# Seven-product gate and up projections in a two-layer trunk, with the weight sums on VectorE

## The chip, the cores and the metric

One core of a Trainium2 chip runs the whole kernel. The metric is the device time of one execution in microseconds; for one core that is its own time. A run's profile gives the span from the first to the last instruction.

## What is computed

A trunk of two layers on 512 tokens with 16 learned meta tokens in front (528 rows of 1024 features, float32). Layer 0 mixes by a state-space scan and a gated linear unit (GLU), layer 1 by windowed attention. Behind each mixer stands a feed-forward network, and it is the object here:

```python
def swiglu_ffn(h, w_gate, w_up, w_down):
    return (jax.nn.silu(h @ w_gate) * (h @ w_up)) @ w_down
# h: (528 or 512, 1024); w_gate, w_up: (1024, 2816); w_down: (2816, 1024)
h_res = h_res + swiglu_ffn(rms_norm(h_res, ln_ffn[i]), w_gate[i], w_up[i], w_down[i])
```

Layer 0 runs it on 528 tokens, layer 1 on 512, since the meta tokens aren't needed behind the attention.

## The kernel before

Activations lie transposed: features on the 128 partitions, tokens along the free dimension. A feature matrix of 1024 rows is 8 blocks of 128. Float32 precision is kept by splitting each operand into a rounded part ("high") and the rest ("low"), and each block product is three matmuls: high x high, low x high and high x low.

**Weights.** SyncE loads a tile of 256 weight columns (all 8 blocks of rows, 1 MB) into one of two buffers `raw` (`load_tile`, line 377; the issue is line 381). ScalarE rounds 128 columns of it into `w_high` (`round_weights`, line 580), VectorE subtracts to make `w_low` (`split_weights`, line 940). Both hold two sets of 128 columns, so the rounding of a set waits until TensorE has finished with the product that used it two products before. SyncE loads a tile when the one before in its buffer is split.

**A quad** is four products: two of gate, two of up (128 output features each). `product` (line 1367) runs over 8 row blocks, three matmuls each; in layer 0 the 528 tokens are cut into 256 and 272 columns in two PSUM banks, in layer 1 a matmul takes all 512. The innermost lines:

```python
for k in range(w_k, w_k + nk):
    for w, xx in ((high, xh), (high, xl), (low, xh)):
        for h, (c0, cn, b0) in enumerate(parts):
            ins = nc.tensor.matmul(banks[:, bank + h, b0:b0 + cn], w[:, j, k, :], xx[...])
```

Feed-forward has 11 quads per layer, in a hardware loop (TensorE lines 1649 to 1660; the layer's input waits are in `first_quad`, line 1633). VectorE (`up`, line 1217) multiplies the gate product by the row of inverse norms, ScalarE (line 812) applies SiLU, GpSimd (line 562) multiplies it by the inverse norm again, for the up product, VectorE multiplies that by the up product out of PSUM. The result is rounded by ScalarE (line 823) and split by VectorE (line 1233) into `a_high`, `a_low`, which hold all 22 blocks.

**The down products** (`down`, lines 1661, 1236 and 825) then give 8 blocks of 128 output features, two at a time, each over the 22 blocks of rows, in four tiles of weights; at the end VectorE adds the product to the residual, and `updated` (lines 776 and 1166) makes the next normed input's high and low parts and the square that the norm needs. The last block of layer 1 is done in two token halves, each with its own addition, scaling and square, and the output transposes follow (lines 1612 to 1631).

**The norm** is taken after the product: `mean` and `spread` (lines 1594 and 1603) are two small groups of matmuls between the first products of a stage; the inverse norm's row is copied out by ScalarE (line 806).

In front of layer 0's feed-forward stand the GLU's four quads (lines 1188 and 1191 multiply and add to the residual). In front of layer 1's stands the output projection of the attention, 8 blocks of 24 matmuls of 512 columns, each followed on VectorE by the addition (line 1351), a weight split and `updated`.

## Time and profile before

| | |
|---|---|
| median of 3 runs | 1182.28 us (1181.73 to 1182.97) |
| span of the profiled execution | 1177.9 us; its own time stands on no page, the median is 4.4 us above the span |
| TensorE busy | 1140.4 us, 97% |
| VectorE busy | 553.8 us, 47% |
| ScalarE busy | 412.4 us, 35% |
| GpSimd busy | 174.8 us, 15% |
| mean granted clock of TensorE | 0.994 |

Matmuls are pipelined: a matmul's length in the trace is its latency, and what it costs is the distance to the next one's start. "Busy" of TensorE is the time in which one is under way. The chain is followed back from the last instruction, at each step to what released it.

### The profile page before, as it was taken

The numbers are of one execution on the slowest core, as the hardware profiler recorded it, in microseconds if no ns is written. First come the engines' busy times: TensorE is split into PE (matmuls) and PEld (weight loads), VectorE is DVE, ScalarE is ACT, GpSimd is POOL, SyncE is SP. The second block draws the span as 40 slices with busy tenths as digits, with TensorE's granted clock in tenths as the row PEclk, the third lists the DMA queues.
The fourth block names the chain that finished last, engine by engine and source line by source line (L and its number), as shares of the span: only waits on it lengthen the run. The fifth ranks groups of instructions, "written<-read, shape, count | busy, mean of one in ns | idle before, by whom it ended". The sixth has DMA issues, their size and how long they took to land.

```text
span 1177.9 us, 20443 instructions
## 1 busy us (share of the span) xinstructions
PE 1140.4 (97%) x8362; PEld 1025.8 (87%) x8362; DVE 553.8 (47%) x845; ACT 412.4 (35%) x701; POOL 174.8 (15%) x114
## 2 busy tenths in 40 slices
PE   5799999999999999999999899989999999999998
PEld 5688899999999999999999676678888888888887
DVE  7978444443344333444334355455443434434444
ACT  6823232332222222233323455443322223223332
POOL 4699000011111111100000000001111111110000
PEclk9999899999999999999999999999999999999999
DMA  7164333222323232222323211022333233223332
GB/s 141 24 163 111 87 109 108 72 89 91 98 80 100 78 107 71 76 83 91 98 81 126 72 37 42 32 72 72 108 107 99 79 107 107 75 73 97 98 98 94
DMA packets 119387, 104.63 MB, mean 89 GB/s; under 512 B 21868, under 2 KB 117216, under 8 KB 119008
## 3 DMA queue, kind: packets, MB, share of 16 engines
q1 hardware_dynamic: 110120, 99.85, 27.9%
q10 hardware_dynamic: 9216, 4.06, 1.5%
q8 instruction: 37, 0.61, 0.2%
q14 instruction: 14, 0.11, 0.0%
HBM read 98.11 MB, written 5.24 MB: 88 GB/s over the span
## 4 chain that ended last, share of the span: by engine, by line
PE 90%; DVE 4%; DMA 2%; ACT 1%; POOL 1%; issue 1%; SPq 0%; ACTq 0%; DVEq 0%; POOLq 0%
PE banks L1380 79%; PE banks L1520 1%; PE banks L1457 1%; PE banks L1510 1%; PE banks L1731 1%; PE banks L1734 1%; PE banks L1752 1%; PE banks L1721 1%; PE banks L1458 1%; DMA y_dram<-y_act 1%; PE banks L1746 1%; PE banks L1472 0%; POOL col_mag L499 0%; PE banks L1720 0%; ACTq L719 0%
## 5 line engine op out<-in xcount | busy, mean ns | idle before, releaser
L587 ACT CAST w_high<-raw 128x1024 fp32r<-128x1024 f32 x186 | 195.0, 1049 | 572.1 <-PE banks L1380 572.1
L945 DVE TENSOR_TENSOR w_low<-raw,w_high 128x1024 fp32r<-128x1024 f32 x186 | 228.2, 1228 | 208.3 <-ACT w_high L587 208.3
L1380 PE MATMUL banks<-x_high,w_high 128*128 128x512 f32 (+2 forms) x1184 | 321.0, 324 | 1.0 <-DVE x_low L1173 1.0
L1380 PE MATMUL banks<-x_high,w_low 128*128 128x512 f32 (+2 forms) x1184 | 318.5, 322 | 0.0
L1380 PE MATMUL banks<-x_low,w_high 128*128 128x512 f32 (+2 forms) x1184 | 317.7, 321 | 0.0
L1380 PEld LDWEIGHTS banks<-x_high,w_high 128*128 128x128 f32 x1184 | 198.9, 189 | 19.4 <-issue 2.2
L1380 PEld LDWEIGHTS banks<-x_low,w_high 128*128 128x128 f32 x1184 | 198.9, 188 | 16.1
L1380 PEld LDWEIGHTS banks<-x_high,w_low 128*128 128x128 f32 x1184 | 198.2, 188 | 16.8
L1380 PE MATMUL banks<-a_high,w_high 128*128 128x256 f32 (+2 forms) x533 | 141.2, 318 | 0.0
L1380 PE MATMUL banks<-a_low,w_high 128*128 128x256 f32 (+2 forms) x533 | 141.1, 318 | 0.0
L1380 PE MATMUL banks<-a_high,w_low 128*128 128x256 f32 (+2 forms) x533 | 141.1, 318 | 0.0
L562 POOL TENSOR_TENSOR gate<-gate,rstd_row 128x528 f32<-128x528 f32 (+1 forms) x44 | 79.3, 1802 | 389.9 <-ACT gate L819 389.9
L1380 PEld LDWEIGHTS banks<-a_low,w_high 128*128 128x128 f32 x533 | 89.3, 188 | 6.8
L1380 PEld LDWEIGHTS banks<-a_high,w_high 128*128 128x128 f32 x533 | 89.3, 188 | 6.7
L1380 PEld LDWEIGHTS banks<-a_high,w_low 128*128 128x128 f32 x533 | 89.2, 188 | 6.6
L1230 DVE TENSOR_TENSOR prod<-banks,gate 128x528 f32<-128x528 f32 (+1 forms) x44 | 30.8, 700 | 131.7 <-PE banks L1380 131.7
L1224 DVE TENSOR_TENSOR gate<-banks,rstd_row 128x528 f32<-128x528 f32 (+1 forms) x44 | 30.6, 699 | 127.8 <-PE banks L1380 120.0
L553 POOL TENSOR_TENSOR rstd<-mean_sq,neg_half 88x6 f32<-88x6 f32 (+1 forms) x3 | 3.7, 1225 | 447.8 <-DVE mean_sq L1201 447.8
L1380 PE MATMUL banks<-glu_high,w_high 128*128 128x256 f32 x224 | 47.6, 294 | 0.7 <-DVE glu_low L1124 0.7
L1380 PE MATMUL banks<-glu_low,w_high 128*128 128x256 f32 x224 | 46.7, 290 | 0.0
L1380 PE MATMUL banks<-glu_high,w_low 128*128 128x256 f32 x224 | 46.4, 289 | 0.0
L1380 PEld LDWEIGHTS banks<-glu_high,w_high 128*128 128x128 f32 x224 | 36.0, 193 | 1.5 <-DVE glu_low L1124 0.9
(288 smaller groups left out, 1249.3 us busy)
## 6 DMA issues: line engine op xcount, KB each, us to landing
raw<-in_ffn_w_gate SPq DMA_DIRECT2D x22, 1024.0 KB, 5.3
raw<-in_ffn_w_up SPq DMA_DIRECT2D x22, 1024.0 KB, 5.3
raw<-in_ffn_w_down SPq DMA_DIRECT2D x16, 768.0 KB, 4.4
raw<-in_ffn_w_down SPq DMA_DIRECT2D x16, 640.0 KB, 4.1
raw<-in_attn_w_qkv SPq DMA_DIRECT2D x6, 1024.0 KB, 5.0
k_toep<-k_dram SPq DMA_DIRECT2D x64, 64.0 KB, 2.6
raw<-in_ssm_w_glu_b SPq DMA_DIRECT2D x4, 1024.0 KB, 5.5
raw<-in_ssm_w_glu_a SPq DMA_DIRECT2D x4, 1024.0 KB, 5.8
```

The costliest lines, as they stand in the source:

```text
L562: nc.gpsimd.tensor_tensor(gate[:, j, a:e], gate[:, j, a:e], rstd_row[:, a:e], ALU.mult).then_inc(gate_scaled, 1)
L587: nc.scalar.copy(high[:, j], raw[:, slot, :, j * P:(j + 1) * P]).then_inc(w_rounded, 1)
L945: nc.vector.tensor_tensor(low[:, j], raw[:, slot, :, j * P:(j + 1) * P], high[:, j], ALU.subtract).then_inc(w_split, 1)
L1224: TT(tokens_of(gate[:, j], n), bank_view(2 * j, n), tokens_of(rstd_row[:], n), ALU.mult).then_inc(pre_ready, 1)
L1230: TT(tokens_of(prod[:, j], n), bank_view(4 + 2 * j, n), tokens_of(gate[:, j], n), ALU.mult).then_inc(up_taken, 1)
L1380: ins = nc.tensor.matmul(banks[:, bank + h, b0:b0 + cn], w[:, j, k, :], xx[:, first_k + k, c0 + base:c0 + base + cn], start=start and k == ...
L1457: nc.tensor.matmul(o, inj[:, r_, i].rearrange("p t q -> p (t q)"), ident[:], start=True, stop=False)
L1458: ins = nc.tensor.matmul(o, inj_t[:, r_, 1 - i].rearrange("p t q -> p (t q)"), (ident if i else neg_ident)[:], start=False, stop=True)
L1510: nc.tensor.matmul(banks[:, 6 + j, r_ * C:(r_ + 1) * C], k_toep[:, b % 2, 2 * r_ + j, :], u_state[:, b * GB + 2 * r_ + j, :], start=True, ...
L1520: ins = nc.tensor.matmul(banks[:, 6 + j, r_ * C + 1:(r_ + 1) * C], read[hs, b % 3, r_, i, 1:T + 1].rearrange("p t q -> p (t q)"), state[hs ...
L1721: ins = nc.tensor.matmul(o[:, META:], q, keys[:, first:first + BAND], start=True, stop=True)
L1731: nc.tensor.transpose(banks[0:w, 6, i * P:(i + 1) * P], prob_b[:, s % 2, i, 0:w], ident[:])
```

## The change

The gate and up products use a seven-product scheme (Strassen's, in Winograd's form). A unit is now 256 weight columns of gate or of up. The weights' row blocks are taken in four pairs, the columns in two blocks of 128, the tokens in two halves (264 or 256), so that each unit is a 2 x 2 by 2 x 2 product of blocks. It takes seven part products of half the tokens instead of eight. Each part is 4 slots x 3 matmuls of 264 or 256 columns.

- Of the weights: five forms of a unit are split into high and low: the first column, S2, the pair S3 and S1, the corner, S4. The four sums are made by VectorE on 512 elements per partition each, two of them in place in `raw`. `raw` has five blocks per pair for it; a unit is loaded by two DMAs of 512 KB.
- Of the inputs: seven forms of each pair of input blocks (`xs_high`, `xs_low`), made as each residual block is ready (`pair_first`, `pair_second`): VectorE makes four differences T1 to T4, ScalarE rounds and VectorE splits all seven.
- Of the results: parts are added by accumulation in PSUM; in between ScalarE copies three states of a bank to SBUF, and VectorE makes three corners from these copies and banks. TensorE waits for a copy before parts 3, 5 and 6 and for a corner before part 7.
- GpSimd's scaling of the gate is gone: VectorE scales the pre-activation by the inverse norm, and the down product once more by it (`scale_down`).
- Activations are kept in 5 slots instead of 22, so the down products are done in three stages (pairs 0 to 2, 3 to 6, 7 to 10), behind 4, 8 and 11 gate and up pairs; each stage adds to the residual. A down unit has two products, with as many matmuls per layer as before. The last unit of layer 1 is done in quarters (two blocks, two token halves).
- The first unit of each layer is prepared while the stage in front of it runs: in layer 0 during the last GLU quad, in layer 1 behind output block 5 (sums and three splits), 6 and 7.
- ScalarE's and VectorE's loops over the quads are written out.

The core of the diff:

```diff
-DOWN_TILES = ((0, 6), (6, 6), (12, 5), (17, 5))
+STAGES = ((0, 3), (3, 7), (7, 11))
+SLOTS = 5
+UPS = ((0, 4), (4, 8), (8, 11))
...
+            def part(w, i, x, slots, c, bank, n, start=False, need=None):
+                for m, slot in enumerate(slots):
+                    if need is not None:
+                        need(m)
+                    for a, b in ((0, 0), (0, 1), (1, 0)):
+                        ins = nc.tensor.matmul(bank_part(bank, n), w[a][:, m, i, :], x[b][:, slot, c, :],
+                                               start=start and m == 0 and a == b, stop=m == len(slots) - 1 and a == 1,
+                                               skip_group_check=not start)
+                ins.then_inc(part_done, 1)
+            def summed_unit(g, ups, downs, parity, x, n, first=False, spread_at=None, mean_at=None, need_b11=None, need_all=None):
+                y, w, v = Y_BANK[parity], W_BANK[parity], X_BANK[parity]
+                forms, slots = 5 * ups + 2 * downs, range(KP)
+                if need_b11 is None and spread_at is None:
+                    pe.wait_ge(set_free, g - 1)
+                pe.wait_ge(t_split, forms + (4 if first else 1))
+                part(col, 0, x, slots, B11, y, n, start=True, need=need_b11)
...
+                part(col, 1, x, slots, B21, v, n, start=True, need=need_all)
+                pe.wait_ge(t_split, forms + (4 if first else 2))
+                pe.wait_ge(part_copied, 3 * ups + 1)
+                part(w2, 0, x, slots, T2, y, n)
...
+                pe.wait_ge(t_split, forms + (5 if first else 3))
+                part(sums, 0, x, slots, T3, w, n, start=True)
+                pe.wait_ge(part_copied, 3 * ups + 2)
+                part(sums, 1, x, slots, T1, y, n)
+                pe.wait_ge(t_split, forms + (5 if first else 4))
+                pe.wait_ge(part_copied, 3 * ups + 3)
+                part(w2, 1, x, slots, T4, w, n)
+                pe.wait_ge(t_split, forms + 5)
+                pe.wait_ge(c22_made, ups + 1)
+                part(w2, 2, x, slots, B22, y, n)
...
+            def sum13(g, kp):
+                TT(w[:, :, 2, :], w[:, :, 4, :], w[:, :, 1, :], ALU.add).then_inc(sums_made, 1)
+                dve.wait_ge(sums_made, 2 * ups_before(g) + 1)
+                TT(w[:, :, 1, :], w[:, :, 1, :], w[:, :, 0, :], ALU.add).then_inc(sums_made, 1)
...
+                TT(s24[:, 0, 0:kp], w[:, :, 0, :], w[:, :, 2, :], ALU.add).then_inc(s2_made, 1)
...
+                TT(s24[:, 1, 0:kp], blocks_of(g, kp)[:, :, 3, :], s24[:, 0, 0:kp], ALU.add).then_inc(s4_made, 1)
...
+                def gate_unit(i, behind):
+                    g, kp = UNITS * layer + up_unit(i), KP
+                    sum2(g + 1, kp)
+                    sum4(g + 1, kp)
...
+                    first_corner(g, gate_part(n, 0, 0))
...
+                    split_column(g + 1, kp)
+                    if behind:
+                        split_acts(i - 1)
+                    split_s2(g + 1, kp)
+                    last_corner(g, gate_part(n, 1, 1))
...
+                    split_sums(g + 1, kp)
+                    low_corner(g, gate_part(n, 1, 0))
...
+                    dve.wait_ge(part_done, parts_before(g) + 7)
+                    TT(gate_part(n, 0, 1), bank_part(Y_BANK[g % 2], n), rstd_part(n, 1), ALU.mult).then_inc(set_free, 1)
+                    dve.wait_ge(c21_made, ups_before(g) + 1)
+                    TT(gate_part(n, 0, 0), gate_part(n, 0, 0), rstd_part(n, 0), ALU.mult)
+                    TT(gate[:, 1, 0:n], gate[:, 1, 0:n], rstd_row[:, t0:L], ALU.mult).then_inc(gate_pre, 1)
+                    split_corner(g + 1, kp)
+                    split_s4(g + 1, kp)
...
+            def pair_second(layer, px, n):
+                dve.wait_ge(xp_ready, 2 * pair + 2)
+                step(STT(x_t[:, 1, 0:h], x_t[:, 0, 0:h], -1.0, x_pair[:, 1, h:n], ALU.mult, ALU.subtract))
+                TT(x_t[:, 2, 0:h], x_pair[:, 0, h:n], x_pair[:, 1, h:n], ALU.subtract)
+                TT(x_t[:, 3, 0:h], x_pair[:, 1, 0:h], x_t[:, 1, 0:h], ALU.add).then_inc(xt_ready, 1)
+                TT(low[:, px, B21:T1, :], ..., high[:, px, B21:T1, :], ALU.subtract).then_inc(xs_split, 1)
+                TT(low[:, px, T1:, :], x_t[:, :, 0:h], high[:, px, T1:, :], ALU.subtract).then_inc(xs_split, 1)
+                square_added(k + 1, n)
...
+                if m == KB - 3:
+                    sum2(UNITS, KP)
+                    sum4(UNITS, KP)
+                    split_s2(UNITS, KP, rounded=1)
+                    split_corner(UNITS, KP, rounded=2)
+                    split_s4(UNITS, KP, rounded=3)
+                if m == KB - 2:
+                    split_column(UNITS, KP, rounded=4)
+                if m == KB - 1:
+                    split_sums(UNITS, KP, rounded=5)
```

TensorE's wait `need_all` in front of each slot of part 2 is for all forms of that pair of inputs. An up unit's queue on VectorE is like the gate unit's without `split_acts`, and its last three products are by the gate. On ScalarE a unit has its three copies, the five roundings of the next unit, and in gate units the rounding of the activations behind `round_s2`, in up units the SiLU of both blocks (1056 or 1024 elements) there.

## Rows read from the trace of the kernel before

**Rows 1.** The summary of the page: busy time per engine, and shares of the chain.

```profile
PE 1140.4 (97%) x8362; PEld 1025.8 (87%) x8362; DVE 553.8 (47%) x845; ACT 412.4 (35%) x701; POOL 174.8 (15%) x114
...
PE 90%; DVE 4%; DMA 2%; ACT 1%; POOL 1%; issue 1%; SPq 0%; ACTq 0%; DVEq 0%; POOLq 0%
```

**Rows 2.** Busy us per engine in stretches of both up stages; then granted clock and DMA.

```profile
250.00:484.00 234.00, 234.00 (x1925) 234.00 (x1925) 91.22 (x101) 65.42 (x83) 38.88 (x22) 1.00 0.28 89
...
830.00:1040.00 210.00, 210.00 (x928) 173.91 (x927) 86.19 (x97) 62.08 (x78) 35.48 (x20) 1.00 0.30 94
```

**Rows 3.** The chain in order of time: start us, us, what.

```profile
247.76 380.39 PE banks L1380 x3120
...
773.76 38.38 PE banks L1380 x168
...
819.41 348.45 PE banks L1380 x1551
```

**Rows 4.** Timeline of TensorE in the last product: start us, us, line, shapes.

```profile
1164.33 0.28 PE L1380 MATMUL banks<-a_high,w_low 128*128 128x256 f32 x1
...
1167.57 0.28 PE L1380 MATMUL banks<-a_high,w_low 128*128 128x256 f32 x1
```

**Rows 5.** Groups by shape of VectorE: count, busy us, mean ns, idle before.

```profile
L945 DVE TENSOR_TENSOR w_low<-raw,w_high 128x1024 fp32r<-128x1024 f32 x186 | 228.2, 1228 | 208.3 <-ACT w_high L587 208.3
...
L1224 DVE TENSOR_TENSOR gate<-banks,rstd_row 128x528 f32<-128x528 f32 x22 | 15.5, 707 | 68.0 <-PE banks L1380 63.9 <-ACT rstd_row L806 4.0
...
L1087 DVE TENSOR_TENSOR nat_b_im<-nat_b_im,lam_t 128x512 f32<-128x512 f32 x1 | 0.7, 693 | 0.0
...
L1137 DVE TENSOR_TENSOR banks<-banks,zt 128x260 f32<-128x260 f32 x8 | 3.5, 437 | 0.3
```

**Rows 6.** Timeline of VectorE in the opening part.

```profile
35.50 0.69 DVE L1087 TENSOR_TENSOR nat_b_im<-nat_b_im,lam_t 128x512 f32<-128x512 f32 x1
36.23 0.69 DVE L1088 TENSOR_TENSOR nat_b_im<-nat_b_im,turn_t 128x512 f32<-128x512 f32 x1
...
37.10 1.22 DVE L1100 TENSOR_TENSOR inj<-banks,nat_b_re 128x1024 f32<-128x1024 f32 x1
38.23 1.22 DVE L1102 TENSOR_TENSOR inj_t<-banks,nat_b_im 128x1024 f32<-128x1024 f32 x1
```

**Rows 7.** Timeline around the end of the GLU products.

```profile
232.34 0.41 PE L1380 MATMUL banks<-x_high,w_high 128*128 128x256 f32 x2
...
232.54 0.71 DVE L1188 TENSOR_TENSOR prod<-banks,gate 128x528 f32<-128x528 f32 x1 [2.79 <-PE banks L1380]
...
233.28 1.27 DVE L1191 TENSOR_TENSOR residual<-residual,prod 128x528 f32<-128x528 f32 x1
...
238.64 0.51 PE L1380 MATMUL banks<-x_high,w_high 128*128 128x256 f32 x2 [0.99 <-DVE x_low L1173]
```

**Rows 8.** Groups by shape of ScalarE.

```profile
L587 ACT CAST w_high<-raw 128x1024 fp32r<-128x1024 f32 x186 | 195.0, 1049 | 572.1 <-PE banks L1380 572.1
...
L890 ACT CAST o_high<-banks 128x256 fp32r<-128x256 f32 x16 | 6.0, 375 | 2.2 <-PE banks L1752 2.2
...
L823 ACT CAST a_high<-prod 128x512 f32 x20 | 12.3, 617 | 0.2 <-issue 0.2
```

**Rows 9.** A DMA issue of the page: KB each, median us to landing.

```profile
raw<-in_ffn_w_gate SPq DMA_DIRECT2D x22, 1024.0 KB, 5.3
```

**Rows 10.** Busy us in slices of 2 us in the attention; the granted clock follows POOL.

```profile
672.00:674.00 2.00, 0.00 (x0) 0.00 (x0) 0.31 (x2) 1.61 (x10) 0.00 (x0) 1.00 0.00 0
674.00:676.00 2.00, 1.12 (x10) 0.90 (x12) 1.78 (x7) 0.00 (x0) 0.00 (x0) 0.87 0.00 0
676.00:678.00 2.00, 2.00 (x10) 1.34 (x7) 0.00 (x0) 1.47 (x7) 0.00 (x0) 0.50 0.03 8
678.00:680.00 2.00, 2.00 (x9) 1.60 (x8) 0.98 (x4) 0.92 (x7) 0.00 (x0) 0.77 0.00 0
```

**Rows 11.** Timeline in the attention: the idle time before is in brackets.

```profile
674.88 0.63 PE L1731 MATMUL banks<-ident,prob_b 128*64 128x128 f32 x4 [3.05 <-DVE prob_m L1327]
```

More of the change, by code:

```diff
@@ L335, in tokens_of @@
             return ap if n == L else ap[:, META:L]
-        def layer_rows(full, short, m, n):
-            return rows(full, m, 0, L) if n == L else rows(short, m, 0, SEQ)
         def cols(ap, n):
@@ L837, in feed_forward @@
                 if layer == 0:
-                    with act.Fori(0, N_DOWN, 1) as i:
-                        down(i, False)
-                else:
-                    with act.Fori(0, N_DOWN - 1, 1) as i:
-                        down(i, False)
-                    for off in range(6):
-                        round_weights(QUAD_DOWN[layer] + 2 * (N_DOWN - 1), 2 + off)
-                    updated(adds0 + KB - 2, KB - 2, n, gain)
-                    for h in range(2):
-                        r_h = half_tokens(h)
-                        act.wait_ge(added, adds0 + KB - 1 + h + 1)
-                        nc.scalar.activation(gate[:, 0, r_h], residual[:, KB - 1, r_h], ACT.Square).then_inc(squared, 1)
@@ L851, in _ @@
-            feed_forward(0, L, N_GLU, KB, 0, "ln_mix1")
+                    for m in range(KB - 2, KB):
+                        normed(m)
+                        squared_of(KB + m, m, n)
+                else:
+                    for q in range(2):
+                        act.wait_ge(last_ready, q + 1)
+                        nc.scalar.activation(last_sq[:, :, q * h:(q + 1) * h], residual[:, KB - 2:, half_tokens(q)],
+                                             ACT.Square).then_inc(squared, 1)
@@ new lines, in plain_product @@
+            def plain_product(x, weights, slots, it0, bank, n, cut, need):
+                for m, slot in enumerate(slots):
+                    if need:
+                        pe.wait_ge(act_split, 2 * (it0 + m) + 2)
+                    for i in range(2):
+                        for a, b in ((0, 0), (0, 1), (1, 0)):
+                            for h, (c0, cn) in enumerate(cut):
+                                ins = nc.tensor.matmul(banks[:, bank + h, 0:cn], weights[a][:, m, i, :], x[b][:, slot, i, c0:c0 + cn],
+                                                       start=m == 0 and i == 0 and a == b, stop=m == len(slots) - 1 and i == 1 and a == 1)
+                ins.then_inc(part_done, 1)
@@ new lines, in plain_unit @@
+            def plain_unit(g, ups, downs, parity, x, s, layer, n):
+                p0, p1 = STAGES[s]
+                slots, it0 = [p % SLOTS for p in range(p0, p1)], N_UP * layer + p0
+                pe.wait_ge(set_free, g - 1)
+                forms = 5 * ups + 2 * downs
+                cut = ((0, TOK), (TOK, TOK)) if n == L else ((0, SEQ),)
+                for j, weights in enumerate((col, sums)):
+                    pe.wait_ge(t_split, forms + j + 1)
+                    plain_product(x, weights, slots, it0, 4 * parity + 2 * j, n, cut, need=j == 0)
@@ new lines, in last_unit @@
+            def last_unit(g, x, s, layer):
+                p0, p1 = STAGES[s]
+                slots, it0 = [p % SLOTS for p in range(p0, p1)], N_UP * layer + p0
+                pe.wait_ge(set_free, g - 1)
+                pe.wait_ge(t_split, forms_before(g) + 2)
+                for q in range(2):
+                    for j, weights in enumerate((col, sums)):
+                        plain_product(x, weights, slots, it0, 4 * (g % 2) + 2 * q + j, SEQ, ((q * SEQ // 2, SEQ // 2),), need=False)
```

784 lines of the change are left out of this document (567 added, 217 removed).

## The prediction

> **What bounds the kernel now.** I read the profile in this order. The summary first [rows 1]: TensorE is busy 97% of the span and carries 90% of the chain that ended last; VectorE is busy 47%. Then busy time by stage [rows 2]: in the gate and up products of both layers TensorE is busy 100% of the stretch, VectorE about 40%, ScalarE under 30%. Then the chain in order of time [rows 3]: one unbroken TensorE piece of 380 us covers layer 0's feed-forward (3120 matmuls, 0.1219 us each), one of 348 us covers layer 1's. Taking 30 matmuls of 256 columns at 0.120 us out of the second (27 steps in 3.24 us [rows 4]), its 1521 of 512 columns take 0.2267 us. So a matmul costs its columns at 2.4 GHz plus about 13 ns, whatever its width. No wait is left in these stages: only fewer columns help, and VectorE has room to pay for them, but how much is the question.
>
> **TensorE's part.** A unit of weights (256 columns of gate or up) costs now, in layer 0, 96 matmuls of 264 columns on average; in layer 1, 48 of 512. After: 7 parts x 4 slots x 3 = 84 of 264 or 256. Layer 0: 22 units x 12 x 0.1219 = 32.2 us less. Layer 1: 1056 x 0.2267 = 239.4 against 1848 x 0.120 = 221.8, 17.6 us less; narrower matmuls give a good part of its one eighth back. The down products keep their matmuls; the last one, cut in quarters, costs 0.4 us more. Together **-49.4 us**. Taking GpSimd's scalings of the gate away gives nothing: they lie beside a TensorE that never waits [rows 2]. Their work comes to VectorE, below.
>
> **VectorE's part, and where the queues meet.** For each unit VectorE now makes five splits (three of 512, two of 1024 elements), four sums of 512, three corners and a last product of half a row. The rows [rows 5]: 1.228 us for 1024 elements, 0.693 for 512, 0.707 for 528, 0.437 for 260. A gate unit has 17 such instructions, the splits of the activations among them, summing to 11.6 us; an up unit 15, 10.1 us. The timeline [rows 6] shows that the next one starts 1.13 us after a 1.22 us one, 0.08-0.09 early, but 0.73 after a 0.69 us one on whose result it waits. Six of the 32 wait so (the sums follow one another). A pair of units then occupies VectorE for 21.7 - 26 x 0.08 + 6 x 0.03 = 19.8 us, against TensorE's 168 x 0.1219 = 20.5 us (layer 0) and 168 x 0.120 = 20.2 (layer 1). VectorE goes from 40% to some 95%.
>
> The Trainium skill speaks against the overlap: "VectorE: DVE Perf Modes", section "The DRAIN you can't avoid", has the next instruction wait until the pipe of the one before is empty. By that rule a pair would take VectorE about 21.9 us, and the whole would be a rival below; [rows 6] say otherwise.
>
> Sums are not in the trace. Below: the 512-element row, 0.61 us apart; above: the residual addition with its permuted operand, 1.27 us for 528 elements against 0.71 [rows 7], so 1.8 times, 1.2 us each. The sums read runs of 128 like the split of row L945, which pays nothing for its gaps, so I take 0.61-0.73.
>
> I laid the three queues of a layer-0 pair beside each other (0: TensorE starts the gate unit; parts of 1.46 us; 0.2 us from a product's end to its reader as in [rows 7], 0.03 between VectorE and ScalarE; ScalarE 1.05 for 1024, 0.38 for a half row, 0.62 for 512 [rows 8]). VectorE comes 2.8 us late, because behind part 7 of the unit before it still has three half or full products and two splits. Sums until 5.6, first corner 5.5-6.0, column split until 7.1, two activation splits until 8.4, split of S2 until 9.0, and only then the corner for which part 7 waits, 8.9-9.3. Part 7 could have started at 8.8; it starts at 9.4. ScalarE rounds the corner's operand (6.5-6.9) well before. An up unit has no activation splits, so its corner comes at 18.9 where part 7 may start at 19.6: it holds nothing. So 0.6 us in each of 16 gate units (0.7 in layer 1), and 0.9-1.0 in the 4 first ones behind a down stage, whose last down unit holds 10 us of VectorE work against 8.8: **+13.9 us**. ScalarE has some 12 us of work per pair (six half-row copies, four of 1024, six of 512, two activation roundings, one SiLU of two rows), and its copies come in time. Weights land 5.3 us after issue [rows 9] and are asked for a whole unit ahead: nothing. The down units hold 5-8 us of VectorE work under 8-12 of TensorE: nothing.
>
> **The starts.** Product 2 of the first unit needs all forms of the last pair of inputs. Layer 0, from the end of the GLU products: product and residual until 2.2 (now 232.54 to 234.55 [rows 7]), VectorE's split of the sums until 3.4 and ScalarE's scaling, three differences until 4.6, ScalarE's rounding of four of them until 5.7, VectorE's split until 7.0. TensorE has work for 2.6 us: it stands 4.5. Unit 1 then waits for the spread of the norm (1.3 us, paid today too) and 1.7 for ScalarE's late copies. In all 8.3 us over the matmuls; today 15.4 us from 232.34 [rows 7] to 247.76 [rows 3] less 96 x 0.1219, 3.7 (1.0 of it the wait at 238.64). **+4.6.**
> Layer 1: the first unit's sums and three splits (4.6 us) and a pair's forms are put into VectorE's queue at output block 5 of 8; that step holds about 11 us and a block lasts 5.45 (24 x 0.2267). All behind is late: from the end of the last output block the residual addition ends at 4.3, and the last split at 9.0; TensorE stands 6.5 in two pieces. With unit 1: 9.7; today 819.41 less 812.14 [rows 3] less 24 x 0.2267, and 0.3 in front, 2.1. **+7.6.**
> Key and value products: the last normed block is ready 6.0 us after the down products (VectorE does a split and a square before the addition) where 5.1 would do: **+0.9.** The tail: both last blocks are scaled, added, squared after the last product, one half-row multiplication (0.4) and a wider square more: **+0.8.**
> Clock: after an idle stretch of TensorE of 3.05 us before 674.88 [rows 11] the granted clock was 0.87, 0.50, 0.77 in three slices of 2 us, the 0.50 being 1.2 of 2.4 GHz [rows 10]: 0.26 + 1.0 + 0.46 = 1.7 us lost. Both starts have an idle stretch of over 4 us: **+3.4.** Bounds: 0 each (the idle 1.0 us before 238.64 [rows 7] is followed by steps at full pace) to about 5 (a longer half-clock stretch).
>
> Sum: -49.4 + 13.9 + 4.6 + 7.6 + 0.9 + 0.8 + 3.4 = -18.2. The profiled span is 1177.9 us; the median of the runs is 1182.28, 4.4 more, which I leave as it is: **1164.1 us**.
>
> **Rivals.**
> A, slower: VectorE becomes the bound of the up stages. A pair has to cost 0.8 us more than the 21.1 (20.8 in layer 1) laid out above and the gain is gone (22 x 0.83 = 18.2); that is VectorE work 8% dearer, 0.05 us on each of 32 instructions. Its place is the corner before part 7, and the waits before it. At 10% dearer the same layout gives 22.3 and 22.1 a pair: +24, 1188 us. For it: instructions in today's trace are mostly alone, the new ones follow one another with two or three waits each. Against: [rows 6]. 0.18.
> B, slower: VectorE instructions in a row do not overlap in the new stages, each starts when the one before has ended: 22.0 and 21.8 a pair, +20, 1184 us. 0.06: [rows 6] contradict it. This is what the rule of the Trainium skill named above would make of the kernel.
> C: VectorE has slack after all, the holds at part 7, half of the starts and the clock's loss vanish: 1164.1 - 13.9 - 7 - 3.4 = 1140; half of that 1152. For it: a handover 0.5 us shorter anywhere in front of the corner ends the hold. 0.08.
> D: no change, 1180 to 1184.7: A in a weaker form. 0.06. That the change doesn't do what it says has no room: the matmuls are written out.
> The forecast: 0.62.
>
> **Numbers.** A measurement of this kernel can tell 0.2%, 2.4 us. Faster: forecast and C, 0.70; same: D, 0.06; slower: A and B, 0.24. The range runs from C's half way, 1150, to a little beyond A, 1190; beyond it lie the whole of C and dearer sums (at 1.2 us each, 2 x 22 x 4 sums x 0.5 = 88 us). The likeliest case alone: 1157 to 1174.
>
> **What would show it.** A unit's seven parts 1.46 us apart in layer 0 and 1.44 in layer 1; VectorE busy over 90% in the up stages; TensorE's idle time in front of part 7 of gate units, released by the corner; idle stretches of 4 us at both starts with a halved clock behind them; pairs of 21.1 and 20.8 us. Wrong would be: pairs over 21.9, idle time in front of other parts, sums over 0.75 us, matmuls more than 0.122 us apart.

## The result and the profile after: 1172.7 us, a gain of 0.7% where 1.5% was forecast

The changed kernel takes 1172.74 us (median of 8 executions, 1163.79 to 1176.3) against 1181.15 (8 executions, 1174.65 to 1182.97): ratio 0.9932, 95% interval 0.9903 to 0.9961, 8.4 us less. The forecast was 1164.1, 18.2 less. The profiled execution took 1163.79 us, nearly the forecast; it is the fastest of the eight, so this agreement is chance, and the account below shows what hid in it. One further execution of before (1196.64 us at a clock of 0.976) ran in a slower state and is left out below.

The summary of the page after, which answers to [rows 1], then busy time in the same two stretches as [rows 2] (columns: TensorE, its weight loads, VectorE, ScalarE, GpSimd, granted clock, DMA share, GB/s):

```profile
PE 1097.6 (94%) x8931; PEld 1018.6 (88%) x8931; DVE 834.1 (72%) x1435; ACT 531.2 (46%) x951; POOL 99.0 (9%) x70
...
PE 77%; DVE 14%; ACT 3%; issue 2%; DMA 1%; POOL 1%; ACTq 0%; SPq 0%; DVEq 0%; POOLq 0%
```

```profile
250.00:484.00 234.00, 228.82 (x1864) 226.99 (x1863) 181.65 (x283) 103.11 (x156) 0.00 (x0) 1.00 0.31 98
830.00:1040.00 210.00, 207.11 (x1418) 192.76 (x1418) 164.33 (x256) 91.43 (x139) 0.00 (x0) 1.00 0.32 100
```

TensorE's share of the chain fell from 90% to 77%, VectorE's rose from 4% to 14%. In the up stages VectorE's busy time doubled and TensorE now has a few us of idle time where it had none.

The chain in order of time, layer 0 and then layer 1, which answers to [rows 3]:

```profile
268.75 11.95 PE banks L2170 x96
284.03 0.71 DVE raw L1478
284.76 0.70 DVE s L1489
286.52 1.04 DVE w_low L1499
287.56 1.32 DVE a_low L1606 x2
289.88 11.96 PE banks L2170 x96
...
827.69 20.42 PE banks L2170 x168
848.57 20.43 PE banks L2170 x168
...
1104.25 32.73 PE banks L2210 x144
1137.00 0.69 DVE gate L1669
1137.70 0.39 DVE scaled L1735
1138.09 1.23 DVE w_low L1504
1139.45 11.75 PE banks L2210 x96
```

The unbroken pieces of 380 and 348 us are gone. A pair of units takes 21.13 us in layer 0 (289.88 less 268.75) and 20.88 in layer 1; in layer 0 the chain leaves TensorE each time for VectorE's sums, splits and activation splits. In front of the last down unit stands a VectorE piece that the forecast does not have.

TensorE's timeline, only matmuls with an idle stretch in front (in brackets, with its releaser):

```profile
234.34 0.59 PE L2170 MATMUL banks<-xs_high,w_high 128*128 128x264 f32 x1 [4.29 <-DVE xs_low L1469]
...
256.41 0.36 PE L2170 MATMUL banks<-xs_high,w_high 128*128 128x264 f32 x1 [2.11 <-ACT parts L1013]
268.75 0.39 PE L2170 MATMUL banks<-xs_high,w_high 128*128 128x264 f32 x1 [0.45 <-DVE gate L1590]
...
787.65 0.36 PE L2170 MATMUL banks<-xs_high,w_high 128*128 128x256 f32 x1 [2.21 <-issue]
...
794.26 0.58 PE L2170 MATMUL banks<-xs_high,w_high 128*128 128x256 f32 x1 [3.86 <-DVE xs_low L1469]
...
815.47 0.36 PE L2170 MATMUL banks<-xs_high,w_high 128*128 128x256 f32 x1 [2.13 <-ACT parts L1013]
...
1139.45 0.36 PE L2210 MATMUL banks<-a_high,w_high 128*128 128x256 f32 x1 [2.49 <-DVE w_low L1504]
```

The holds at part 7 (20 like that at 268.75, 0.42 to 0.48 us), and the idle stretches of both starts (4.29; 2.21 and 3.86) are where the forecast has them. Those at 256.41, 815.47 and 1139.45 are larger than forecast or not in it.

**Two figures for every kernel.** Each execution lists its span and TensorE's mean granted clock. I call span x (1 - clock) the clock lost, and span x clock the time at full clock. The second scatters far less (a standard error of 0.1 to 1.1 us here) and so measures edits that the median hides. It is not quite the time without throttling: half-clock time in which TensorE had nothing to do counts as lost and costs nothing. Executions of one kernel get 0.5 to 1.0 us longer per us lost, 0.69 fitted to all kernels together. So the time at full clock comes out some 0.3 us lower for each us that a kernel loses more, and two kernels compare well by it only where they lose about the same. Clock lost and time at full clock are means over the executions; ratios are those of medians to the kernel before in the same runs:

| kernel | executions | median us | ratio (95%) | clock lost | at full clock |
|---|---|---|---|---|---|
| before, all runs | 70 | 1177 to 1181 | 1 | 8.9 | 1168.3 |
| after, first runs | 8 | 1172.74 | 0.9932 (0.9903, 0.9961) | 17.4 | 1153.0 |
| after, again | 10 | 1170.78 | 0.9944 (0.9916, 0.9972) | 15.9 | 1153.7 |
| filled | 5 | 1166.76 | 0.9912 (0.9875, 0.9948) | 8.2 | 1156.9 |
| filled, again | 6 | 1170.21 | 0.9903 (0.9873, 0.9932) | 12.3 | 1155.6 |
| acts_later | 4 | 1157.62 | 0.9836 (0.9796, 0.9877) | 13.9 | 1142.2 |
| last_column | 4 | 1167.73 | 0.9893 (0.9832, 0.9955) | 15.5 | 1150.5 |
| silu_later | 4 | 1169.68 | 0.9897 (0.9837, 0.9958) | 15.2 | 1151.8 |
| starts | 10 | 1170.58 | 0.9921 (0.9894, 0.9948) | 17.8 | 1150.7 |
| sum_twice | 10 | 1187.50 | 1.0069 (1.0040, 1.0098) | 16.7 | 1168.8 |
| all | 6 | 1153.08 | 0.9781 (0.9751, 0.9811) | 16.5 | 1134.3 |
| all_filled | 6 | 1149.40 | 0.9764 (0.9736, 0.9793) | 13.0 | 1135.2 |
| before_idle | 6 | 1192.40 | 1.0101 (1.0080, 1.0123) | 17.3 | 1174.4 |

The change is worth 14.9 us at full clock (1168.3 less 1153.4, the mean over all 18 executions), where the forecast without its clock term is 21.6; and it loses 7.7 us more clock (16.6 against 8.9), where the forecast has 3.4. Since the two kernels lose different amounts, 14.9 flatters the change. Brought to no loss with 0.69 us per us, an estimate from these executions, before takes 1171.1 us and after 1158.6: 12.5 us less, of which the 7.7 us of clock cost 5.3. Both ways the means of the spans differ by 7.2 us.

### The profile page after: what moved, and what is told of

Its sections match the earlier page's. It is cut to its first block, busy times and chain, and to the rows that moved or that the text cites. A ratio compares the mean times of both kernels' runs of the same rounds, so it can differ in the third digit from the quotient of the medians.

```text
span 1162.0 us, 22259 instructions
## 1 busy us (share of the span) xinstructions
PE 1097.6 (94%) x8931; PEld 1018.6 (88%) x8931; DVE 834.1 (72%) x1435; ACT 531.2 (46%) x951; POOL 99.0 (9%) x70
## 3 DMA queue, kind: packets, MB, share of 16 engines
q10 hardware_dynamic: 9216, 4.06, 1.5%
## 4 chain that ended last, share of the span: by engine, by line
PE 77%; DVE 14%; ACT 3%; issue 2%; DMA 1%; POOL 1%; ACTq 0%; SPq 0%; DVEq 0%; POOLq 0%
PE banks L2170 30%; PE banks L2210 21%; PE banks L1891 15%; PE banks L2031 1%; PE banks L1968 1%; DVE a_low L1606 1%; PE banks L2021 1%; PE banks L2307 1%; DVE w_low L1499 1%; PE banks L2310 1%; DVE raw L1478 1%; DVE s L1489 1%; PE banks L2328 1%; PE banks L2297 1%; PE banks L1969 1%
## 5 line engine op out<-in xcount | busy, mean ns | idle before, releaser
L2170 PE MATMUL banks<-xs_high,w_high 128*128 128x264 f32 (+1 forms) x1232 | 354.3, 288 | 25.1 <-DVE gate L1590 9.1
L2170 PE MATMUL banks<-xs_low,w_high 128*128 128x264 f32 (+1 forms) x1232 | 350.4, 284 | 0.0
L2170 PE MATMUL banks<-xs_high,w_low 128*128 128x264 f32 (+1 forms) x1232 | 350.3, 284 | 0.0
L2170 PEld LDWEIGHTS banks<-xs_high,w_high 128*128 128x128 f32 x1232 | 235.3, 191 | 31.6 <-DVE gate L1590 13.2
L2170 PEld LDWEIGHTS banks<-xs_low,w_high 128*128 128x128 f32 x1232 | 235.7, 191 | 0.1
L2170 PEld LDWEIGHTS banks<-xs_high,w_low 128*128 128x128 f32 x1232 | 235.3, 191 | 0.0
L2210 PE MATMUL banks<-a_high,w_high 128*128 128x264 f32 (+2 forms) x544 | 143.2, 316 | 2.5 <-DVE w_low L1504 2.5
L2210 PE MATMUL banks<-a_high,w_low 128*128 128x264 f32 (+2 forms) x544 | 142.9, 315 | 0.0
L2210 PE MATMUL banks<-a_low,w_high 128*128 128x264 f32 (+2 forms) x544 | 142.7, 315 | 0.0
L1218 DVE TENSOR_TENSOR w_low<-raw,w_high 128x1024 fp32r<-128x1024 f32 x34 | 41.5, 1222 | 40.1 <-ACT w_high L694 40.1
L1514 DVE TENSOR_TENSOR w_low<-raw,w_high 128x1024 fp32r<-128x1024 f32 x44 | 53.8, 1222 | 10.1 <-ACT w_high L949 10.1
```

Source lines behind the costliest of these rows:

```text
L1218: nc.vector.tensor_tensor(low[:, j], tile_of(slot)[:, :, j * P:(j + 1) * P], high[:, j], ALU.subtract).then_inc(w_split, 1)
L1514: TT(sum_high(w_low, kp), blocks_of(g, kp)[:, :, 1:3, :], sum_high(w_high, kp), ALU.subtract).then_inc(t_split, 1)
L2170: ins = nc.tensor.matmul(bank_part(bank, n), w[a][:, m, i, :], x[b][:, slot, c, :], start=start and m == 0 and a == b, stop=m == len(slots ...
L2210: ins = nc.tensor.matmul(banks[:, bank + h, 0:cn], weights[a][:, m, i, :], x[b][:, slot, i, c0:c0 + cn], start=m == 0 and i == 0 and a == ...
```

## Experiments

### Both kernels again, for their clocks

No edit.

> The kernel after the change, unchanged, for a second profile and its clocks. Its profiled execution took 1163.8 us at a mean granted clock of 0.994, its seven others 1171.9 to 1176.3 at 0.981 to 0.985. Clock theory: the instructions and their waits are those of the profile in hand (pairs of 21.1 and 20.9 us), and what the usual execution has more is one or more stretches at half clock, worth 0.010 of 1170 us, 12 us of clock, that is some 20 us at 1.2 GHz; a profile at 0.984 then shows them in the slices, behind the two idle starts or in the state-space part. Rival: a profile at 0.984 has its 9 us in longer pairs or longer waits of VectorE, and the clock only falls because TensorE stands more. Expected: 1172 median; a profile between 1171 and 1176 or again one of 1164.

> The kernel before the change, unchanged, for the clocks of its executions, which decide how much of the difference is clock. Its profiled execution had 0.994 and 1177.9 us of span with a half-clock stretch of some 10 us in the state-space part. Clock theory: most executions show 0.991 to 0.994, against 0.984 of the changed kernel, so that the usual execution after loses 5 to 9 us more to the clock than the usual one before. Rival: the executions of before show 0.984 too; then the clock is no part of the difference and the 9 us lie elsewhere. Expected: 1181 us.

Measured: after 1170.78 us with 0.980 to 0.994, 15.9 us of clock lost; before 1179.24 (the 20 executions beside them: 1177.11) with 0.988 to 0.998, 9.0 and 8.7 lost. The profile of after has 0.986 this time, the same pairs (21.13), the same idle stretches, and more half-clock time. The stretch of layer 1's start in slices of 6 us, in the first profile of after and in the second (busy TensorE, then granted clock, DMA share, GB/s):

```profile
790.00:796.00 6.00, 2.14 (x12) 0.84 0.56 175
796.00:802.00 6.00, 6.00 (x47) 0.88 0.00 0
```

```profile
796.00:802.00 6.00, 4.16 (x20) 0.59 0.48 165
802.00:808.00 6.00, 6.00 (x32) 0.56 0.00 0
```

6 x (0.16 + 0.12) = 1.7 us are lost in the first, 6 x (0.41 + 0.44) = 5.1 in the second, behind the same idle stretch. So the rival (longer pairs) falls, and the clock theory holds, though only half of the loss lies at the starts: of the 10.2 us of clock that this profile lost more than the first (17.6 against 7.4 in windows of 5 us), 5.1 lie behind the two starts and 5.1 in the attention. There the kernel before scatters too, with 1.7 us lost in its first profile and 5.1 in its second. One thing in my expectation was wrong: before's executions lie between 0.988 and 0.998, not within 0.991 to 0.994; the two profiled executions with which I began happened to have the same clock, 0.994. The second profile of before also loses clock at layer 0's start, behind the idle stretch of 0.98 us that the first has as well (0.99 us, then full clock):

```profile
240.00:242.00 2.00, 2.00 (x19) 0.73 0.47 155
242.00:244.00 2.00, 2.00 (x11) 0.50 0.00 0
```

### Filling the two idle starts

```diff
+            def fill(layer, x, n, count):
+                for _ in range(count):
+                    nc.tensor.matmul(bank_part(W_BANK[0], n), col[0][:, 0, 0, :], x[0][:, 0, B11, :], start=True, stop=True)
...
-                            need_b11=lambda m: pe.wait_ge(xs_split, 3 * (KP * layer + m) + 1),
-                            need_all=lambda m: pe.wait_ge(xs_split, 3 * (KP * layer + m) + 3))
+                            need_b11=lambda m: need(layer, x, n, m, 1, 16 if layer == 1 else 0),
+                            need_all=lambda m: need(layer, x, n, m, 3, 30))
```

(`need` makes `count` matmuls for the last pair of inputs, and waits.)

> The changed kernel with matmuls of no use in TensorE's idle stretches at the two starts: 30 in front of the last pair of inputs in product 2 of each first unit (30 x 0.12 = 3.6 us of the 4.29 and 3.86 idle), and 16 more in layer 1 in front of the last pair of product 1 (1.9 of 2.21 idle). They go to a bank that is overwritten. If the usual 9 us are half-clock stretches behind these idle stretches, this runs at a mean clock of 0.990 or more and takes 1160 to 1164 in most executions (also without the two stretches of 3.4 us, 1.7 each, that the profile has). If the low clock comes from elsewhere (the state-space part or the attention), it stays at 1169 to 1173 with 0.985. If VectorE and not TensorE sets the starts, nothing but the clock may change: any loss over 1 us would be the matmuls themselves.

> The changed kernel with the idle stretches of both starts filled by matmuls of no use, once more and with more executions, beside the control above on one chip. Before, five executions lost 8.2 us of clock in the mean against 16.6 of the changed kernel. Clock theory: 8 to 10 lost again, median 1164 to 1167. Rival (the five were luck, as the later filled version with 13.0 lost could suggest): 13 or more, median 1169 or more.

Measured: 8.2 us lost, against 8.7 of the kernel before in the same runs; then 12.3, against 11.3 of the kernel before, which lost more in those runs too. Both times the excess over before is within 1 us (each mean of clock lost has a standard error of 2.5 us), where the changed kernel's is 7.2 (15.9 less 8.7). The second absolute figure missed my 8 to 10; compared with its own runs it fits. The first profile in the same slices, layer 0's start and layer 1's:

```profile
234.00:240.00 6.00, 5.34 (x48) 1.00 0.34 97
...
796.00:802.00 6.00, 6.00 (x53) 1.00 0.00 0
```

No half clock at either start. One idle stretch was not filled, that of 2.21 us in layer 1: it stands in front of the first pair of inputs, and the 16 matmuls meant for it came behind it.

```profile
786.41 0.36 PE L2170 MATMUL banks<-xs_high,w_high 128*128 128x256 f32 x1 [2.21 <-issue]
...
787.55 2.08 PE L2238 MATMUL banks<-xs_high,w_high 128*128 128x256 f32 x16
```

The second set's profile loses no clock behind the filled stretches and 1.7 us at 260, behind unit 1's idle stretch of 2.12 us, which was not to be filled. The 16 matmuls only delay: the matmul that waits for the last inputs starts 10.3 us behind the output products (794.51 less 784.21) in place of 8.8 in after (794.26 less 785.45). So the median gains less than the clock. The time at full clock rose by 2 to 3.5 us, and part of that is the figure itself; brought to no loss as above, both filled sets take 1159.5 us, 0.9 more than the changed kernel.

### The counter-test: idle starts in the kernel before

```diff
+                    if i == N_GLU - 1 and j == 1:
+                        for _ in range(5):
+                            step(TT(prod[:, 0], prod[:, 1], prod[:, 1], ALU.mult))
                     updated(2 * i + j, 2 * i + j, L, "ln_ffn0")
...
+                if m == KB - 1:
+                    for _ in range(8):
+                        step(TT(prod[:, 0], prod[:, 1], prod[:, 1], ALU.mult))
                 updated(2 * KB + m, m, SEQ, "ln_ffn1")
```

> The kernel before, with work of no use on VectorE in front of the last input's split at both starts: 5 multiplications of 528 elements, each waiting for the one before (0.73 us apart) in layer 0, 8 in layer 1. TensorE, which stood 1.0 us in layer 0 and not at all in layer 1, then stands some 4.4 us in each (3.5 and 4.4 more). If idle stretches of this length at these two places are what lowers the clock of the changed kernel, this one loses 15 us of clock in the mean of its executions where the kernel before loses 8.5, and its median is 7.9 us of idle time plus 5 to 6 of clock, 13 to 14 us, over that of before, 1191. Forecast's price (one short half-clock stretch each, 1.7 us): 11 us over, 1188 to 1189, 12 lost. Rival (the clock of the changed kernel falls for what its feed-forward stages do, narrow matmuls and holds of 0.5 us): 8 us over, 1185.5, and 8.5 lost.

Measured: 1192.40, 11.3 us over the 1181.15 beside it; 17.3 us lost against 11.3. The profile's slices behind the two idle stretches (3.75 and 4.30 us by its timeline):

```profile
240.00:246.00 6.00, 6.00 (x31) 0.50 0.01 3
...
826.00:832.00 6.00, 6.00 (x17) 0.50 0.01 3
```

So 6.0 us more clock lost (17.3 with a standard error of 1.8, against 11.3 with 0.9), from idle time alone, in a kernel without seven-product units and without their holds. Of the three, the rival that lays it on the feed-forward stages (8.5 lost) is refuted. The median came out at the forecast's price (11 us over), the clock lost nearer to the other (15 expected from 8.5, so 6.5 more). The means say more than the median here: the mean span rose by 12.9 us, 6.9 at full clock and 6.0 of clock, close to the theory's 13 to 14.

### The holds at part 7

```diff
                     split_column(g + 1, kp)
-                    if behind:
-                        split_acts(i - 1)
                     split_s2(g + 1, kp)
                     last_corner(g, gate_part(n, 1, 1))
+                    if behind:
+                        split_acts(i - 1)
```

> In each gate unit the two activation splits (2.4 us of VectorE) are moved from in front of the corner that part 7 waits for to behind it. Forecast's theory (hold at part 7, 13.9 us in all): the holds of 0.5 to 1 us vanish, pairs go from 21.1 to 20.4 to 20.6 us in layer 0 and from 20.9 to 20.2 to 20.4 in layer 1, and the kernel takes 9 to 13 us less than the changed one, some 1161 against 1172.7. Rival (VectorE is the bound, and the hold only shows its lag): a pair stays at 20.9 or more, with the idle time in front of another part, and the time falls by less than 4 us.

Measured: 11.2 us less at full clock, 1157.62 us. The waits of TensorE for the corner (us in total, times, longest), after and then here, and the chain here from unit 2 to the first down stage:

```profile
PE banks L2170 <- DVE gate L1590: 9.1, 20, 0.5
```

```profile
PE banks L2170 <- DVE gate L1590: 1.8, 4, 0.5
...
255.98 64.44 PE banks L2170 x528
```

Sixteen of the 20 holds are gone (16 x 0.7 is the 11.2 measured), and the three pairs run in one piece, 0.1220 us a matmul. The four left are behind a down stage, where no activation split stands in the gate unit's queue. VectorE's total work was not the bound; the order of its queue was. The rival falls.

```diff
                     sum2(g + 1, kp)
+                    dve.wait_ge(s2_made, ups_before(g + 1) + 1)
+                    mark(TT(s24[:, 1, 0:kp], blocks_of(g + 1, kp)[:, :, 3, :], s24[:, 0, 0:kp], ALU.add))
+                    dve.wait_ge(dve_step, steps[0])
                     sum4(g + 1, kp)
```

> One sum of 512 elements is made twice in each gate unit: 0.7 us more of VectorE in each pair, nothing else. Forecast's theory (VectorE's work in front of the corner is on the path of part 7, one for one; its pair of 19.8 us has 0.6 to 0.7 us left under TensorE's 20.5 and 20.2): the hold grows from 0.45 to 1.15 us, pairs go from 21.13 to 21.85 and from 20.88 to 21.6, 20 x 0.7 = 14 us more. Rival A in its full form (VectorE bounds the whole pair): the same 0.7, but with idle time in front of other parts as well. Rival C (slack): under 0.3 a pair, 6 us.

Measured: 15.4 us more at full clock. TensorE's timeline has the same 20 holds, 0.7 longer (23.3 us in all where after has 9.1), and no other:

```profile
296.05 0.39 PE L2173 MATMUL banks<-xs_high,w_high 128*128 128x264 f32 x1 [1.17 <-DVE gate L1590]
```

One 0.7 us addition per pair would have made the change a loss of 0.7% (1.0069). That is the size of rival A's extra work, and it shows how narrow the forecast's margin was.

### The waits that the forecast missed

The last down unit (`last_unit`):

```diff
-                pe.wait_ge(t_split, forms_before(g) + 2)
                 for q in range(2):
                     for j, weights in enumerate((col, sums)):
+                        if q == 0:
+                            pe.wait_ge(t_split, forms_before(g) + j + 1)
```

> The profile after shows a hold that the forecast does not have: TensorE stands 2.49 us in front of the last down unit (1139.45), released by the split of its second form, because that unit waits for both forms at its head. Here it waits for the first form alone at its head and for the second before the product that reads it, 24 matmuls (2.9 us) later. Theory (a missed term of 2.5 to 2.7 us): the hold falls to under 0.3 us and the stretch from the end of the unit before to the end of the last product from 14.4 to 11.9 us, nothing else changes, the kernel gains 2.5 us. Rival (the split only comes later because the additions before it are late, or the tail is set by VectorE): the wait appears again in front of the second product or behind the last one, and the end moves by less than 1 us.

Measured: 2.9 us less at full clock (standard error of the difference 1.2). In the profile the idle stretch of 2.49 us is gone; from VectorE's read of the last product before it to the end of the last product it is 11.48 us (1142.45 to 1153.93), where after has 14.21 (1137.00 to 1151.21). The rival falls.

The first SiLU of each layer, on ScalarE:

```diff
-                    silu(i)
+                    if i > 0:
+                        silu(i)
                     copy_last(g)
+                    if i == 0:
+                        silu(i)
```

> In unit 1 of each layer ScalarE's copy for part 6 is queued behind the first SiLU, which waits for the gate of a late unit 0 and for its table load (1.28 us from one to the other); TensorE stands 2.11 and 2.13 us there. Here the first SiLU comes behind that copy. Theory (another missed term, 1.7 us per layer): the two idle stretches of 2.1 us vanish, or shrink to the 0.4 us of an ordinary hold, and the stretch of two units behind each start gets 1.7 to 2.1 us shorter; 3.5 to 4 us in all. Rival: VectorE, a unit behind, then waits for the SiLU with its product, and the same 2 us come back as a longer hold in unit 2 (over 2 us in front of its part 7 in place of 0.45): less than 1 us gained.

ScalarE's timeline of after says why: the table load and the SiLU stand in front of the copy for part 6 (L1013).

```profile
253.62 1.28 ACT L1018 ACT_TABLE_LOAD   x1
254.91 1.08 ACT L1018 ACTIVATE gate<-gate 128x1056 f32<-128x1056 f32 x1
255.90 0.36 ACT L1013 COPY parts<-banks 128x264 f32<-128x264 f32 x1
```

Measured: half of it. The 2.11 became 0.41, but TensorE then waits 0.32 in front of part 6 of the next unit and 0.60 in place of 0.45 at part 7. At full clock 1.6 us less (standard error of the difference 0.7, four executions), where 3.5 to 4 were expected: theory and rival are both partly right, since VectorE is still a step behind in unit 2.

### The starts

```diff
-                if m == KB - 1:
-                    split_sums(UNITS, KP, rounded=5)
                 if m % 2 == 0:
...
+                if m == KB - 4:
+                    sum2(UNITS, KP)
+                    sum4(UNITS, KP)
+                if m == KB - 1:
+                    split_sums(UNITS, KP, rounded=5)
```

(The pair's own work now comes ahead of these; the three splits of block 5 go to block 6; layer 0's `split_sums` goes behind `pair_second`; ScalarE likewise.)

> The work for the first unit is moved out of the way of the last inputs: in layer 1 its four sums go from output block 5 to block 4, three splits from block 5 to block 6, and in both layers the split of the two sums goes behind the last inputs' splits, on both engines. Forecast's theory (the starts cost what VectorE's queue holds in front of the last inputs): TensorE's idle time falls from 6.1 us in two pieces to 3 to 3.5 in one in layer 1, and from 4.3 to about 3 in layer 0, 4 us less in all; and if the usual loss by the clock follows the length of these idle stretches, the mean clock goes up from 0.985 too, by another 2 to 6 us. Rival: the starts stay as long because the chain through ScalarE (five steps from the last addition) sets them: less than 1.5 us. A third: the split that is put back holds part 4 instead, idle time there of over 1 us.

```profile
237.71 0.39 PE L2169 MATMUL banks<-xs_high,w_high 128*128 128x264 f32 x1 [4.06 <-DVE xs_low L1468]
...
794.48 0.35 PE L2169 MATMUL banks<-xs_high,w_high 128*128 128x256 f32 x1 [0.33 <-issue]
...
800.79 0.39 PE L2169 MATMUL banks<-xs_high,w_high 128*128 128x256 f32 x1 [3.56 <-DVE xs_low L1468]
```

Layer 1: 6.07 us of idle time became 3.89. Layer 0: 4.29 became 4.06, as the second theory has it; there the chain through ScalarE sets the start, not the queue: VectorE itself now waits for ScalarE twice in front of it, 0.80 and 0.59 us. The time at full clock fell by 2.7. The clock did not gain (17.8 lost): idle stretches of 4.06 and 3.56 us cost as much clock as those of 4.29 and 3.86.

### Together

> The four edits together: activation splits behind the last corner, the last down unit's second form waited for late, the first SiLU behind the copy for part 6, the first units' sums and splits out of the way of the last inputs. By the holds that their own profiles show: 20 x 0.65 (the hold and its restart) = 13, last unit 2.5, unit 1 about 1.9 (3.5 of waits less 1.6 that came back as two holds in front of parts 6 and 7), starts 2.4. If these are separate places, the time less the clock lost (span x mean clock, mean over the executions) falls from 1153.4 to 1134 to 1137, and the median to 1148 to 1153 with a clock of 0.985. If they share one slack of VectorE (what one gives back another holds), it stays over 1140.

> The same with matmuls of no use in the one idle stretch of each start (30 of 264 columns in layer 0, 27 of 256 in layer 1, to a bank that is overwritten). Clock theory: the two starts are where the new kernel loses 7 us of clock where the one before loses about 1; without the idle stretches the mean clock lost falls from 16 or 17 us of an execution to 8 or 9, as much as the kernel before loses, and the median is 5 to 7 us under the one without them, 1142 to 1147. Rival (the clock of an execution is the chip's, and the first filled kernel's 0.994 was luck in five executions): both medians agree within 2 us and the clocks too.

The edits of acts_later, last_column, silu_later and starts add up: 19.1 us at full clock, where the four runs alone give 18.4 (11.2 + 2.9 + 1.6 + 2.7). The kernel takes 1153.08 us, 2.2% under before, and the filled version 1149.40, 2.4%, the fastest of the study. Filling gained 3.7 us and 3.5 of clock, not the 8 expected: the executions still lose 13.0, where before lost 7.8 beside them. Its profile shows no loss at the starts; it has 5.1 us near 130, 1.7 and 3.4 in the attention and its output products, 1.6 at the end, places that the other profiles have as well. Whether these lose more in this kernel, or six executions are too few, stays open. Brought to no loss, the two kernels agree (1139.4 and 1139.3), so by this measure the filling saved clock and did nothing else.

## Why the prediction was off: one term sized too low, two waits left out

The profiled executions compared stage by stage, before and after, all by their timelines:

| stage | change, us | forecast |
|---|---|---|
| up to the end of the GLU products (232.54, now 227.55) | -5.0 | 0 |
| layer 0's feed-forward, up to the first key and value sums (395.6, now 379.4) | -16.3 | -18.3 |
| key and value products to the attention's end (178.4 both) | 0 | 0 |
| layer 1's, from the end of the output products (361.3, now 365.9) | +4.6 | -0.7 |
| tail (10.0, now 10.8) | +0.8 | +0.8 |

The first row is no part of the change. The profiled execution of before ran at half clock near 132 to 144 us and lost 5.1 us; the first one after did not, though other profiles after do (starts, sum_twice, all). The forecast's base was slightly off as well: it took the median of three executions, 1182.28, where 70 have a median of 1179.2. That moves the forecast time by 3 us and leaves the forecast change as it is.

**TensorE's part, -49.4: right.** 84 matmuls a unit at the same pace: 0.122 us in layer 0, 0.120 in layer 1, so 168 give 20.5 and 20.2 us. Narrower matmuls gave back what was laid out.

**VectorE's part: right.** The groups of VectorE after, by shape:

```profile
L1478 DVE TENSOR_TENSOR raw<-raw 128x512 f32<-128x512 f32 x44 | 30.5, 693 | 1.5
L1489 DVE TENSOR_TENSOR s<-raw 128x512 f32<-128x512 f32 x44 | 30.5, 692 | 1.5
...
L1499 DVE TENSOR_TENSOR w_low<-raw,w_high 128x1024 fp32r<-128x1024 f32 x60 | 73.0, 1217 | 5.7 <-ACT w_high L937 5.5
```

The sums cost 0.69 us and start 0.72 apart (284.03, 284.76), within the 0.61 to 0.73 taken; the upper bound of 1.2 did not arise. A pair in layer 0 occupies VectorE for 19.7 us, 93% of its 21.13, where 19.8 us were forecast, some 95% of the time; the 182 us of 234 above are an average with the down stages. Rival B did not arise either. VectorE's timeline:

```profile
288.80 0.69 DVE L1509 TENSOR_TENSOR w_low<-s,w_high 128x512 fp32r<-128x512 f32 x1
289.40 0.42 DVE L1590 TENSOR_TENSOR gate<-parts,banks 128x264 f32<-128x264 f32 x1
289.74 1.22 DVE L1514 TENSOR_TENSOR w_low<-raw,w_high 128x1024 fp32r<-128x1024 f32 x1
290.88 0.43 DVE L1596 TENSOR_TENSOR gate<-banks,parts 128x264 f32<-128x264 f32 x1
```

Instructions that do not wait for the one before start 0.08 to 0.09 us ahead of its end in the new stages too. The Trainium skill ("VectorE: DVE Perf Modes", "The DRAIN you can't avoid") says that the next instruction does not start until the pipe is empty, and adds that one that is not held starts earlier. The forecast named the first half alone, as rival B; the trace agrees with the second.

**The holds, +13.9: right.** Twenty, at the corner before part 7. With the restart each costs 0.65 us in layer 0 (21.13 less 168 x 0.1219) and 0.7 in layer 1, some 13.6 in all. Those behind a down stage are no longer than the others (0.42 to 0.46 us), not the 0.9 to 1.0 forecast; the forecast's own counts add up to 14.0 to 14.4, not 13.9. acts_later took away 11.2 of it, sum_twice lengthened it one for one.

**The starts, +4.6 and +7.6: place right, size low by 1.5 and 1.7.** The first idle stretches are as forecast (4.29 for 4.5; 6.07 for 6.5). Short was unit 1: "1.7 for ScalarE's late copies" were 0.68 and 2.11 with two restarts, because the copy stands behind the first SiLU, and that behind its table load of 1.28 us, which I had not looked for.

**Left out: the last down unit, 2.7 us.** I costed its extra matmuls and not its wait. It asks for both forms at its head, and ScalarE starts to round the second only at 1137.00, when the product in front has read that buffer. last_column shows it.

**The key and value products, +0.9: too much.** TensorE stands 0.30 us there (605.90), some 0.5 with the restart.

**The clock, +3.4: the step that failed by its size.** I took one short half-clock stretch for each start, 1.7 us, from the single case in the attention [rows 10], and kept up to 5 us each as a bound. The lower bound, no loss behind 1.0 us of idle time [rows 7], was one execution's luck too: the second profile of before loses 1.7 us there. Eight profiles of kernels with idle starts show, from the granted clock in windows of 5 us, 1.6 to 6.8 us lost at layer 0's start with unit 1 (mean 3.8) and 1.6 to 5.2 at layer 1's (mean 3.4). The kernel before lost 0 and 1.7 there in its two profiles. So the typical execution loses 5.5 to 7.2 us more there than before, not 3.4. The executions say 7.7 in all; making the stretches in the old kernel brings 6.0; filling them takes the excess away in two sets of runs and leaves 5.2 us of 8.7 in the third (all_filled), whose profile loses nothing at the starts.

The balance: 21.6 forecast without clock less 1.5, 1.7 and 2.7, and 0.4 more for the key and value products, is 16.1. Measured are 14.9 at full clock and, brought to no loss, 12.5; so 1.2 to 3.6 us are not placed. The clock costs the rest: 7.7 us lost, 5.3 of time by the slope, for the 3.4 forecast. That leaves 7.2 us between the mean spans, 8.4 between the medians of the first runs. So the size of the clock term is one failed step of three; the unit 1 and last-unit waits, 5.9 us together, weigh about as much. The rivals: A and B did not come true; C's "a handover 0.5 us shorter anywhere in front of the corner ends the hold" is what acts_later made of it by hand.

## What to carry to other kernels

When a change makes a saturated engine wait in a new place, price the clock behind each idle stretch by several executions of the old kernel, not by one profile: one execution's clock differed here by as much as the change was worth. Compare kernels by span times granted clock, where edits of 2 to 3 us just show in four executions, but only kernels that lose about the same clock; otherwise fit what a lost us costs first. And when a helper engine has slack but the main engine still stands, look at what is queued in front of the one result it waits for: moving two instructions behind two others gave back 11.2 us at full clock, where the whole scheme had gained 8.4 in the medians.

## What the hardware showed that I had not expected

Behind equal idle stretches of about 4 us, TensorE's clock was halved for different lengths: losses came as about 1.7, 3.4 or 5.1 us (layer 1's start: 1.7 three times, 3.4 twice, 5.1 three times in the eight profiles), and idle stretches cut from 4.3 and 3.9 to 4.06 and 3.56 us made no difference. Even unit 1's idle stretch of 2.1 us was followed by a loss of 1.7 us in some profiles (at 255 to 265 us in the second one of after) and by none in the first. Behind an idle stretch of 1.0 us the kernel before lost 1.7 us in one profile and nothing in the other. A us of clock lost did not cost a us of time: between the two profiles of after, layer 0's feed-forward lost 1.7 us more and took 1.0 longer, layer 1's lost 3.4 more and took 2.8 longer.
